# Gate and value projections of a two-block model: high and low inputs streamed together as 512 columns

## The reference

```python
v = rmsnorm(h, g_ffn[i]) @ w_up[i]          # 1024 -> 2 x 2816
v = causal_dwconv(v, ffn_conv_w[i], ffn_conv_b[i])   # 3 taps
v_gate, v_val = jnp.split(v, 2, axis=-1)
h = h + (jax.nn.gelu(v_gate) * v_val) @ w_down[i]    # 2816 -> 1024
```

## Time and profile before

| | |
|---|---|
| median of 3 runs | 883.9 us (882.26 to 888.82) |
| the profiled execution | 886.84 us, its span 885.0 us |
| mean granted TensorE clock | 0.984 |
| TensorE busy | 858.9 us (97%), 7055 matmuls |
| VectorE, ScalarE, POOL busy | 559.5, 486.1, 628.4 us |
| gate and value stage | about 661 to 779 us |

### The profile page before, as it was taken

One profiled execution on the slowest core, in us unless ns is written; L12 is line 12 of the kernel. 1 busy time (PEld: TensorE's weight loads), 2 busy tenths in 40 slices (PEclk: granted clock), 3 DMA queues, 4 the chain that ended last, 5 costly groups with the idle time before them and its releaser, 6 DMA issues.

```text
span 885.0 us, 18293 instructions
## 1 busy us (share of the span) xinstructions
PE 858.9 (97%) x7055; PEld 825.3 (93%) x7055; DVE 559.5 (63%) x1541; ACT 486.1 (55%) x923; POOL 628.4 (71%) x282
## 2 busy tenths in 40 slices
PE   8999999999999999999999989889999999999995
PEld 8999988889998899999999988768999999999995
DVE  5997758764344486775369987665556666641164
ACT  6754476655446565655555566655554444554351
POOL 3999656656986556654977997344767888889681
PEclk9999999999999999999999998989999999999997
DMA  9677533333765335342757575232555666667511
GB/s 333 199 219 216 179 117 86 105 84 102 227 193 169 101 110 162 102 144 70 217 169 212 168 222 184 72 99 78 166 172 168 191 190 188 174 191 226 177 48 49
DMA packets 38678, 138.85 MB, mean 157 GB/s; under 512 B 4416, under 2 KB 4416, under 8 KB 38592
## 3 DMA queue, kind: packets, MB, share of 16 engines
q1 hardware_dynamic: 38592, 137.69, 51.4%
HBM read 136.63 MB, written 1.05 MB: 156 GB/s over the span
## 4 chain that ended last, share of the span: by engine, by line
PE 74%; POOL 4%; DVE 4%; ACT 3%; issue 2%; POOLq 0%; ACTq 0%; DVEq 0%
PE ps L612 20%; PE ps L613 20%; PE ps L614 20%; POOL wl L558 4%; ACT wh L1099 1%; PE ps L834 1%; PE ps L639 1%; PE ps L740 1%; PE ps L657 1%; PE ps L994 1%; PE ps L967 1%; PE ps L858 1%; PE ps L830 1%; PE ps L805 1%; PE ps L722 1%
## 5 line engine op out<-in xcount | busy, mean ns | idle before, releaser
L558 POOL TENSOR_TENSOR wl<-raw,wh 128x1024 fp32r<-128x1024 f32 x254 | 611.1, 2432 | 214.2 <-ACT wh L1099 214.0
L612 PE MATMUL ps<-uh,wh 128*128 128x256 f32 x1248 | 354.1, 284 | 3.0 <-DVE wl L1623 1.6
L614 PE MATMUL ps<-uh,wl 128*128 128x256 f32 x1248 | 350.2, 281 | 0.0
L613 PE MATMUL ps<-ul,wh 128*128 128x256 f32 x1248 | 350.0, 280 | 0.0
L1099 ACT ACTIVATE wh<-raw 128x1024 fp32r<-128x1024 f32 x256 | 264.6, 1054 | 86.2 <-PE ps L614 79.1
L612 PEld LDWEIGHTS ps<-uh,wh 128*128 128x128 f32 x1248 | 235.8, 189 | 4.8 <-issue 2.3
L613 PEld LDWEIGHTS ps<-ul,wh 128*128 128x128 f32 x1248 | 236.2, 189 | 0.0
L614 PEld LDWEIGHTS ps<-uh,wl 128*128 128x128 f32 x1248 | 235.7, 189 | 0.0
L1777 DVE TENSOR_TENSOR h<-ps,h 128x256 f32<-128x256 f32 x32 | 13.6, 425 | 106.3 <-PE ps L614 106.1
L614 PE MATMUL ps<-ffh,wl 128*128 128x256 f32 x176 | 49.3, 280 | 0.0
L612 PE MATMUL ps<-ffh,wh 128*128 128x256 f32 x176 | 49.1, 279 | 0.0
(11 more groups left out here) (359 smaller groups left out, 1733.8 us busy)
## 6 DMA issues: line engine op xcount, KB each, us to landing
raw<-slabs SPq DMA_DIRECT2D x256, 512.0 KB, 4.0
h<-x_fm SPq DMA_DIRECT2D x4, 256.0 KB, 5.5
out_fm<-outb SPq DMA_DIRECT2D x4, 256.0 KB, 2.2
cst<-shape_consts SPq DMA_DIRECT2D x1, 768.0 KB, 9.3
vec<-vectors SPq DMA_DIRECT2D x1, 299.5 KB, 9.4
pin<-p_fm SPq DMA_DIRECT2D x1, 256.0 KB, 4.0
vec<-vectors SPq DMA_DIRECT2D x1, 4.0 KB, 2.5
```

Source lines behind the costliest of these rows:

```text
L558: nc.gpsimd.tensor_tensor(wl[:, s % PART_RING, :], raw[:, s % RAW_RING, :], wh[:, s % PART_RING, :].bitcast(f32), ALU.subtract).then_inc(s ...
L612: nc.tensor.matmul(res, w_h, a_h, start=first, stop=False)
L613: nc.tensor.matmul(res, w_h, a_l, start=False, stop=False)
L614: ins = nc.tensor.matmul(res, w_l, a_h, start=False, stop=last)
```

## The change

For the jobs `fg` and `fv` the high and low inputs are two halves of one tensor (`u2`). For each k TensorE streams both, 512 columns, against the high weight: the high part's product goes to the left half of the output bank and the low part's to the right half. A second matmul of 256 columns adds low weight by high input to the left half. ScalarE copies the right half to a new tile `flow` (two buffers), VectorE adds it to the left half in PSUM, waits for its own addition, and takes the tile as before. In `add_to_residual` the addition into `h` is moved behind `add_square(n, k - 1)`; its two-halves branch is for tiles in `TWO_HALVES`, which holds `fg` and `fv` only.

```diff
+TWO_HALVES = {"fg": KF, "fv": KF}
...
-        uh, ul = ar("uh", [KD, T], f32r), ar("ul", [KD, T], f32r)
+        u2 = ar("u2", [2, KD, T], f32r)
+        uh, ul = u2[:, 0], u2[:, 1]
...
             def project_part(name, hi, lo, k0, k1, ready=None):
+                both = {"so": yn2, "mo": og2, "wo": m2, "fd": ff2, "fg": u2, "fv": u2}.get(name[:2])
...
-                        if j.kind == "F":
+                        if j.kind == "F" and two_halves(name):
+                            nc.tensor.matmul(halves(o), w_h, both[:, :, k, :], start=first, stop=False)
+                            ins = nc.tensor.matmul(o[:, 0:T], w_l, hi(k), start=False, stop=last)
+                        elif j.kind == "F":
...
+            def ff_half(c):
+
+                o = output(f"f{'gv'[c % 2]}{c // 2}")
+                wait(act, "ff_sum", c - 1)
+                nc.scalar.activation(flow[:, c % 2, :], o[:, T:2 * T], ACT.Copy).then_inc(sem("ff_half"), 1)
...
             for i in range(KF):
-                for s in "gv":
-                    feed(f"f{s}{i}")
+                ff_half(2 * i)
+                ff_half(2 * i + 1)
                 if i:
                     ff_high(i - 1)
                 ff_act(i)
...
                 for k in range(KD):
                     o = output(f"{prefix}{k}")
-                    tt(h[:, k, :], o[:, 0:T], h[:, k, :], ALU.add).then_inc(sem("dve_evac"), 1)
+                    if two_halves(f"{prefix}{k}"):
...
                     if k:
                         add_square(n, k - 1)
+                    if two_halves(f"{prefix}{k}"):
+                        dve.wait_ge(sem("low_added"), low_added[0])
+                    tt(h[:, k, :], o[:, 0:T], h[:, k, :], ALU.add).then_inc(sem("dve_evac"), 1)
                     taken(f"{prefix}{k}")
...
             def take_ff(c):
                 if c >= 4:
                     dve.wait_ge(sem("ff_tap"), 2 * FF_TAPS * ((c - 4) // 2 + 1))
+                o = output(f"f{'gv'[c % 2]}{c // 2}")
+                dve.wait_ge(sem("ff_half"), c + 1)
+                tt(o[:, 0:T], o[:, 0:T], flow[:, c % 2, :], ALU.add).then_inc(sem("ff_sum"), 1)
+                dve.wait_ge(sem("ff_sum"), c + 1)
                 take(f"f{'gv'[c % 2]}{c // 2}", fraw[:, c % 4, FF_TAPS - 1:])
```

More of the change, by code:

```diff
@@ L175, with two_halves @@
         "w_o_nsa_2": 4, "w_out_2": 8, "w_up_2": 8, "w_down_2": KF, "w_ple_gate_2": 8, "w_ple_2": 2}
+def two_halves(name):
+    return name[:2] in TWO_HALVES and int(name[2:]) < TWO_HALVES[name[:2]]
 class Job:
@@ L322, in build @@
         phase()
-        uh, ul = ar("uh", [KD, T], f32r), ar("ul", [KD, T], f32r)
+        u2 = ar("u2", [2, KD, T], f32r)
+        uh, ul = u2[:, 0], u2[:, 1]
         after_u = cursor[0]
-        ynh, ynl = ar("ynh", [16, T], f32r), ar("ynl", [16, T], f32r)
+        yn2 = ar("yn2", [2, 16, T], f32r)
+        ynh, ynl = yn2[:, 0], yn2[:, 1]
         xs, bT, cT = ar("xs", [16, T]), ar("bT", [8, T]), ar("cT", [8, T])
@@ L345, in build @@
         phase(after_u)
-        ogh, ogl = ar("ogh", [16, T], f32r), ar("ogl", [16, T], f32r)
+        og2 = ar("og2", [2, 16, T], f32r)
+        ogh, ogl = og2[:, 0], og2[:, 1]
         vn = ar("vn", [TB, MLA_H * P])
@@ L387, in build @@
         npn, npT = ar("npn", [4, 3 * P]), ar("npT", [2, 3 * P])
-        mh, ml = ar("mh", [KD, T], f32r), ar("ml", [KD, T], f32r)
+        m2 = ar("m2", [2, KD, T], f32r)
+        mh, ml = m2[:, 0], m2[:, 1]
         phase(after_u)
-        ffh, ffl = ar("ffh", [KF, T], f32r), ar("ffl", [KF, T], f32r)
+        ff2 = ar("ff2", [2, KF, T], f32r)
+        ffh, ffl = ff2[:, 0], ff2[:, 1]
         fraw = ar("fraw", [4, T + FF_TAPS - 1])
         fge = ar("fge", [2, T])
+        flow = ar("flow", [2, T])
         pin = ar("pin", [2, T])
@@ L625, in project_part, with halves @@
                         ins.then_inc(sem("slab_done"), 1)
+            def halves(o):
+                return o[:].rearrange("p (a t) -> p a t", a=2)
             def norm_sum(n):
@@ L1764, in _ @@
             gained_before = {n.i: KD * i for i, n in enumerate((n_mla, n_mix, n_ffn, n_ple))}
+            low_added = [0]
             def add_to_residual(prefix, n):
@@ L1776, in add_to_residual @@
                     o = output(f"{prefix}{k}")
-                    tt(h[:, k, :], o[:, 0:T], h[:, k, :], ALU.add).then_inc(sem("dve_evac"), 1)
+                    if two_halves(f"{prefix}{k}"):
+                        low_added[0] += 1
+                        tt(h[:, k, :], o[:, T:2 * T], h[:, k, :], ALU.add).then_inc(sem("low_added"), 1)
                     if k:
                         add_square(n, k - 1)
+                    if two_halves(f"{prefix}{k}"):
+                        dve.wait_ge(sem("low_added"), low_added[0])
+                    tt(h[:, k, :], o[:, 0:T], h[:, k, :], ALU.add).then_inc(sem("dve_evac"), 1)
                     taken(f"{prefix}{k}")
```

## The result

The changed kernel takes 907.08 us (median of 4 runs, 905.86 to 908.0) against 885.16 for the kernel before (4 runs): a ratio of 1.025, interval 1.0224 to 1.0275, or 21.9 us slower. The profiled execution has a span of 904.0 us against 885.0.

A forecast was written before the change was run, and what follows sets the result against it. Bound before: TensorE, 5.65 us a pair; after: a ScalarE-VectorE loop of 6.62. The stage's 19.1 us plus 0.6 for the moved addition make 19.7, so 903.6 us on the median 883.9; range 895 to 914.

The forecast's parts named there:

- TensorE's part almost nothing: Gate and value stage: a k step takes 0.351 us against 0.354, since the removed weight load was already hidden.
- The term of 0.9 us: TensorE's saving over 352 k steps of 0.0025 us each, if TensorE still sets the pace; none of it kept.
- The loop: Gate and value stage: a cycle between ScalarE and VectorE of 6.62 us a pair, 0.97 over TensorE's 5.65.
- The start: Beginning of the gate and value stage: VectorE starts at 661.56, first Gelu at 665.24 instead of 664.31.
- The end: Last Gelu 20.96 us later; fd0's slack of 1.9 is consumed first, so 19.1 us reaches the down projection.
- The moved addition: Four add_to_residual calls: 0.13 us later in three and 0.24 in one, 0.6 in sum, bounds 0 and 2.4.
- Rival 3, the clock: Gate and value stage: stalls lower TensorE's clock to half for half the stage, 52 us more, 955; chance 4%.

The follow-up runs named there:

- the stream alone: Changed kernel with the 512 + 256 column matmuls but without ScalarE's copy and VectorE's addition of the right half: 883.99 us, ratio 1.0002 to the kernel before.
- the old order: Changed kernel with the addition into h put back ahead of the square sum in all four residual additions: 905.52 us, ratio 1.0236 to the kernel before.
- the take-out alone: Changed kernel with three 256-column matmuls per k step again, high-by-low into the right half; copy, addition and wait kept: 904.95 us, ratio 1.0238 to the kernel before.

## Why the prediction was right

The forecast was 903.6 us on a median of 883.9, 19.7 us or 2.2% more; measured were 21.9 us and 2.5%.

- *TensorE's part almost nothing.* Right, shown by the stream alone. The term of 0.9 us was still too large: 0.353 us a step either way. The Trainium skill's 131 ns for 512 columns ("TensorE: Matmul & The Clock Gate", section "Back-to-back issue gap") has no counterpart: here the 512-column matmul is followed after 0.23 us (712.21 to 712.44).
- *The loop.* Right in mechanism and size: 6.64 measured, 6.62 forecast; its pieces 3.04 on ScalarE to the value addition (3.01 forecast), 3.09 from there to the fifth tap (3.09), 0.51 to the Gelu (0.52). Within ScalarE's part two errors nearly cancel, which is luck: the copy was dearer at its end (0.51 to the value addition, not 0.42) and cheaper before the next feed (0.26, not 0.33). Taking one and then both feeds off, placing one between, and lengthening the copy gave 6.22, 5.65 (TensorE's), 5.71 and 7.48.
- *The start.* The first Gelu comes 3.68 us after VectorE's first operation (659.12 to 662.80), as forecast (661.56 to 665.24).
- *The end.* Two of fd0's last steps wait for VectorE's low part, as forecast (0.35 and 1.13 us). The size was off by what follows.
- *The moved addition.* 0.13 at wo seen; the last low part at mo comes 446.10 - 443.58 = 2.52 after the release, and was 445.62 - 443.37 = 2.25 in the trace before: 0.27, forecast 0.24. At wo it reaches the norm's factor: VectorE's copy into `late` comes 6.69 us after the release (651.70 to 658.39), and 6.57 in the kernel before (654.33 to 660.90) and with the old order (650.78 to 657.35). What reaches the end of the kernel stays open.
- *Rival 3, the clock.* In the stage itself the stalls did not lower it: 1.00 throughout. But it did fall behind the stage, which I had not priced. TensorE's timeline at the end of fd0, and the stretches there (length, busy, granted clock, DMA share, GB/s):

```profile
802.18 0.39 PE L628 MATMUL ps<-ff,wh 128*128 128x256 f32 x1 [0.35 <-DVE ff L2187]
...
803.94 0.47 PE L628 MATMUL ps<-ff,wh 128*128 128x256 f32 x1 [1.13 <-DVE ff L2187]
804.21 0.42 PE L629 MATMUL ps<-ff,wh 128*128 128x256 f32 x1
804.43 0.42 PE L630 MATMUL ps<-ff,wl 128*128 128x256 f32 x1
```

```profile
802.00:804.00 2.00, 0.69 (x4) 1.00 0.66 223
804.00:807.00 3.00, 3.00 (x14) 0.51 0.30 113
```

After being busy 0.69 of 2 us, TensorE's granted clock is at its lower level (0.51; 1.2 GHz) for some 3 us (1.00 again from 808), with a matmul of 256 columns every 0.21 us instead of 0.118: about 15 matmuls x 0.096 = 1.4 us. The trace of the take-out alone, whose clock stayed at 1.00 there, has 7.77 us from fd0's result to fd1's (804.26 to 812.03); that of the old order, where it fell to 0.72 in 804 to 810, has 9.29 (804.09 to 813.38): 1.5 us. So this comes in some executions and not in others.

The profiled spans add up so. From VectorE's first operation on wo's last tile to fd0's result, the changed kernel takes 805.53 - 651.70 = 153.83 us, the one before 787.39 - 654.33 = 133.06: 20.8 more, against 19.1 forecast. From there to the end it is 0.9 more, clock included. Up to wo it is 2.6 less, which is not the change's doing (below). 20.8 + 0.9 - 2.6 = 19.1, the difference of the spans within rounding; without the 2.6 it is 21.7, beside 21.9 between the medians.

Of the 1.7 above the forecast, 0.2 lies ahead of the stage (7.42 us from wo's last tile to VectorE's first operation, 651.70 to 659.12, and 7.23 before, 654.33 to 661.56), 0.12 of it the moved addition. About 0.5 is a second omission: ScalarE's copy of `ph` (0.62 us) in one of the pairs lies on the loop too, and that pair's period is 7.16 (782.10 to 789.26). Another 0.5 is 19 x 0.03, since the other full periods are 6.65 in the mean, not 6.62. The last 0.4 is fd0's end, with the slower clock in it: 2.97 us from the last Gelu to fd0's result (802.56 to 805.53), where the forecast's times give 1.91 to the last step and, as before, 0.69 from there (786.7 to 787.39).

## What to carry to other kernels

Before adding a stage to a take-out, write down what stands ahead of it in its engine's queue, and whether that work waits, by any path, for the engine it will release: then the price is what the length of the cycle exceeds the pace by, whatever the engine's busy share. The two 0.4 us copies of a pair cost nothing or 12 or 22 us in all here, by their place among the two feeds. And the wider matmul gave back nothing for 352 weight loads, which were already hidden; the spacing of matmuls at two widths in the trace of before (0.456 and 0.460 ns a column) had told that.

## What the runs showed of the hardware that I had not expected

The clock in a stretch that no kernel here changes differs between executions. The same stretch, 550 to 600 us, for the kernel before, the changed kernel and the take-out alone (busy of the five engines, then granted clock):

```profile
550.00:600.00 50.00, 43.36 (x342) 37.72 (x341) 31.22 (x104) 27.71 (x82) 18.98 (x8) 0.88 0.32 96
```

```profile
550.00:600.00 50.00, 43.00 (x366) 38.01 (x366) 32.75 (x110) 29.03 (x85) 19.56 (x10) 0.95 0.31 96
```

```profile
550.00:600.00 50.00, 42.11 (x371) 37.34 (x370) 33.12 (x111) 29.75 (x86) 20.38 (x10) 1.00 0.32 96
```

With 0.88, 0.95 and 1.00 there, the profiled kernels reach wo's last tile at different times (654.33 and 651.70 for the first two), although the changed kernel is the slower up to there by its moved additions. The other traces and runs bear this out. In the twelve profiled executions the last square sum of wo starts at 650.8 to 652.3 us where the granted clock of 445 to 650 us was 0.99 or 1.00 (three of them), at 652.2 to 654.3 where it was 0.98 (five), and at 655.7 to 657.7 where it was 0.96 (four), though at mo's last tile they are within 1.2 us of each other. And of 23 executions of the kernel before on one chip, the four with a mean granted clock of 0.995 took 879.8 to 883.2 us, the six with 0.984 to 0.986 took 886.0 to 889.9. So the 7 to 10 us by which repeated executions of one kernel spread go with the clock. Why it differs from one execution to the next stays open.
